# One row-maximum instruction over both score maps of a unit instead of two, in the first attention stage

## The reference, cut to what matters

```python
k1a, k2a = jnp.split(k_all, 2, axis=-1)
sa = DA ** -0.5
oa = attend(q1, k1a, v_all, sa) - lam.astype(hn.dtype) * attend(q2, k2a, v_all, sa)
# attend, per block of 128 queries:
s = jnp.einsum('bhqd,bhkd->bhqk', qblk, k).astype(jnp.float32) * scale
p = jax.nn.softmax(s, axis=-1).astype(v.dtype)
return jnp.einsum('bhqk,bhkd->bhqd', p, v)
```

## Time and profile before

| what | value |
|---|---|
| median of three runs | 2000.77 us (1998.8 to 2004.0) |
| span of the profiled execution | 2001.7 us |
| TensorE busy, whole span | 1921.7 us (96%) |
| VectorE busy, whole span | 1071.2 us (54%) |
| ScalarE busy, whole span | 717.5 us (36%) |
| the maxima of line 1415 | 60, of which 40 in the first attention stage |

### The profile page before, as it was taken

The page is one execution under the profiler, slowest core; times in us unless marked ns, Lnnn a source line. Parts: engine busy times, 40 slices in busy tenths (PEclk is TensorE's granted clock), DMA queues, the critical chain, the costliest instruction groups (busy, mean ns, idle before and its releaser), DMA issues.

```text
span 2001.7 us, 41374 instructions
## 1 busy us (share of the span) xinstructions
PE 1921.7 (96%) x18397; PEld 1700.8 (85%) x18397; DVE 1071.2 (54%) x1976; ACT 717.5 (36%) x1313; POOL 140.2 (7%) x138
## 2 busy tenths in 40 slices
PE   5998999999999999999999889999999999999997
PEld 2795444899999999999998678888659999999997
DVE  3226754475555563245475776766547555556223
ACT  2323554353333351133345744444214333334211
POOL 2000000000000000000001523322000000000000
PEclk7999999999999999999999999999899999999999
DMA  9123738312221223232221000000211222122322
GB/s 339 56 85 119 273 112 301 119 58 85 85 70 58 85 58 87 59 105 70 64 84 41 7 3 4 4 4 4 91 43 43 85 84 84 52 76 59 87 64 76
DMA packets 142065, 164.25 MB, mean 82 GB/s; under 512 B 2512, under 2 KB 107136, under 8 KB 141888
## 3 DMA queue, kind: packets, MB, share of 16 engines
q1 hardware_dynamic: 138736, 150.29, 23.3%
q0 software_dynamic: 3152, 11.32, 1.5%
HBM read 157.85 MB, written 3.75 MB: 81 GB/s over the span
## 4 chain that ended last, share of the span: by engine, by line
PE 87%; DVE 6%; DMA 2%; POOL 2%; ACT 1%; issue 1%; POOLq 0%; DVEq 0%; SPq 0%
PE ps L226 82%; DMA ring<-in_ada_w 2%; POOL work L2786 1%; PE ps L2422 1%; DVE ring L2671 1%; PE ps L1280 1%; DVE work L498 1%; POOL work L2788 1%; PE ps L347 1%; PE ps L2027 1%; DVE small L1415 0%; PE ps L2400 0%; PE ps L462 0%; DVE work L2689 0%; DVE work L2684 0%
## 5 line engine op out<-in xcount | busy, mean ns | idle before, releaser
L226 PE MATMUL ps<-x_hi_r,w_lo 128*128 128x320 f32 (+3 forms) x2240 | 519.7, 307 | 0.4 <-issue 0.4
L226 PE MATMUL ps<-x_hi_r,w_hi 128*128 128x320 f32 (+2 forms) x1792 | 428.9, 311 | 0.9 <-issue 0.9
L226 PE MATMUL ps<-x_lo_r,w_hi 128*128 128x320 f32 (+2 forms) x1792 | 424.9, 308 | 0.0
L226 PEld LDWEIGHTS ps<-x_hi_r,w_lo 128*128 128x128 f32 (+1 forms) x2240 | 372.4, 186 | 2.0 <-issue 0.5
L226 PEld LDWEIGHTS ps<-x_lo_r,w_hi 128*128 128x128 f32 x1792 | 305.6, 188 | 0.0
L226 PEld LDWEIGHTS ps<-x_hi_r,w_hi 128*128 128x128 f32 x1792 | 303.8, 188 | 1.4 <-issue 1.3
L226 PE MATMUL ps<-work 64*64 64x64 f32 (+9 forms) x3322 | 285.0, 281 | 17.0 <-ACT work L1344 6.7
L226 PEld LDWEIGHTS ps<-work 64*64 64x64 f32 (+5 forms) x3322 | 177.7, 152 | 97.6 <-issue 64.1
L678 DVE SCALAR_TENSOR_TENSOR work<-ps,par,work 128x511 f32<-128x511 f32 (+1 forms) x188 | 103.3, 550 | 254.5 <-ACT work L840 244.6
L840 ACT ACTIVATE work<-ps,par 128x640 f32<-128x640 f32 x88 | 78.0, 886 | 372.5 <-PE ps L226 372.5
L718 ACT ACTIVATE w_hi<-ring 128x1024 fp32r<-128x1024 f32 (+1 forms) x152 | 135.8, 938 | 206.9 <-DMA ring<-in_ffn_down 182.7
(11 more groups left out here) (383 smaller groups left out, 2534.1 us busy)
## 6 DMA issues: line engine op xcount, KB each, us to landing
ring<-in_ada_w SPq DMA_DIRECT2D x24, 2048.0 KB, 8.1
ring<-in_ffn_up SPq DMA_DIRECT2D x44, 1024.0 KB, 7.3
ring<-in_ffn_down SPq DMA_DIRECT2D x16, 1408.0 KB, 6.9
ring<-in_l_w_in SPq DMA_DIRECT2D x11, 1024.0 KB, 5.2
ring<-in_l_w_out SPq DMA_DIRECT2D x4, 2048.0 KB, 7.9
ring<-in_l_w_in SPq DMA_DIRECT2D x3, 2048.0 KB, 9.5
h<-in_xT POOLq DMA_DIRECT2D x1, 2560.0 KB, 14.7
out_yT<-work POOLq DMA_DIRECT2D x2, 768.0 KB, 4.0
```

Of the source, the lines that this page charges most:

```text
L226: return pe.matmul(out, lhsT, rhs, start=first, stop=last)
```

## The change

In the first attention stage one `tensor_reduce` takes the maxima of both maps of a unit: it reads PSUM as 128 x 2 x w (w is 640 or 128), reduces the innermost axis and writes two neighbouring columns of `small`, the same ones as before. It waits for the scores of both maps and raises the semaphore by two at its end. The waits on ScalarE stay as they are. In the second stage nothing changes.

```diff
+            def both_maxima(u):
+                w = NT if units[u][1] < 4 else P
+                dve.wait_ge(sg(x + "scores"), 2 * u + 2)
+                c = 32 + (2 * u % 4)
+                maps_at = ps_all[:, 0:2048].rearrange("p (s n) -> p s n", s=2)[:, :, 0:w]
+                dve.tensor_reduce(small[:, c:c + 2], maps_at, AXX, ALU.max, negate=True).then_inc(sg(x + "max"), 2)
+
...
             for u in range(len(units)):
-                maximum(u, 0)
                 if g == 0:
-                    maximum(u, 1)
+                    both_maxima(u)
                     weigh(u, 0)
                     weigh(u, 1)
                 else:
+                    maximum(u, 0)
                     weigh(u - 1, 0)
```

## The result

The changed kernel took 2010.57 us, median of four runs (2006.85 to 2011.73), against 2000.99 for four runs of the kernel before: ratio 1.0047, 95% interval 1.0034 to 1.006. It is slower by about 9.6 us; 8.4 were forecast. The time lies in the range.

The account below looks back on a forecast made before the run. A ring of three engines, once round per unit, was taken to bound the stage. Twelve latent units 8.04, unit 2 0.26 and unit 4 0.14 gave +8.4 us: 2000.77 + 8.4 = 2009.2, range 2004.8 to 2012.5.

Parts of the forecast that it names:

- The ring, and the first maximum on it: First stage: scores, maxima and exponentials go round three engines once per unit, 3.96 us; only the first maximum lies on the path.
- The duration: Time of the new joint maximum on VectorE: 1.49 us over 1280 columns, 0.42 us in context units.
- d: How much later a latent unit's first exponential starts: 1.49 - 0.82 = 0.67 us.
- The wait for both maps: Before the joint maximum: waiting for both maps' scores rather than the first's costs almost nothing.
- Unit 2: TensorE there waits for the ring's weights; 0.41 us of slack leaves 0.67 - 0.41 = 0.26 us of loss.
- Units 7, 12, 17, and 9, 14, 19: First three hidden by a ScalarE copy, by 0.05 us; 9 and 14 by TensorE's transposes; no scores follow 19.
- The sum: Loss over the first stage: 8.04 + 0.26 + 0.14 = +8.4 us, bounds +4.8 and +10.8.
- Rival B: Scores stand behind TensorE's own queue, so the lateness is hidden: not slower, 2000.8 us at full cover; chance 0.15.
- twelve uncovered units: Latent units 0, 1, 3, 5, 6, 8, 10, 11, 13, 15, 16, 18: 12 x 0.67 = 8.04 us.
- Rival C: VectorE's queue sets the period, so fewer instructions win 1.4 us: 1999.4 us, no measurable change; chance 0.03.
- Rival D: TensorE idles more, its granted clock falls to 0.94 in the stage, 4.9 us more: 2014.1 us; chance 0.07.
- A: The forecast itself: late first exponential in the first stage, +8.4 us, 2009.2 us; chance 0.75.

Follow-up runs that it names:

- The move of the copy: ScalarE copies the previous head's context result between the two exponentials of units 7, 12, 17: ratio 0.9998 on the kernel before, 1.0048 on the changed kernel.
- the filling: Changed kernel with the transposes of units 0 to 4 done twice (ratio 1.0072), then three times (one run, 2009.7 us).

## Why the prediction was right, step by step

*The ring, and the first maximum on it.* Shown. Taking the early signal away costs the loss by itself; taking the maximum twice costs another 1.53 us in every latent unit at the full clock. The engine that lost work, VectorE, lost it off the path.

*The duration.* 1.49 and 0.42 forecast, 1.492 and 0.416 measured. d = 0.67 held.

*The wait for both maps.* Mis-sized: "costs almost nothing" was 0.11 us in each latent unit, 0.04 for the second map's scores and 0.07 for the wait as an instruction of its own, which the raise by two brings. The prediction had read the end of the last matmul off a row, and those ends are modelled: 0.04 us can't be read there. I had read the cost of the change from the instruction that it adds and not from how it signals. Twelve units make 1.3 us of it.

*Unit 2.* 0.26 forecast, 0.41 in the first profile, and 0.78 where the weights come in time, as they did in the other profiles. Slack against a transfer was counted on from a single execution.

*Units 7, 12, 17, and 9, 14, 19.* Covered, as forecast; the first three by so little that the 0.11 us cost 0.05 each. The move of the copy shows what covers them.

*The sum.* +8.4 forecast, +10.0 in the stage at the full clock. What is missing is 12 x 0.11 = 1.3, 0.15 and 0.15. That the runs' 9.6 us lie so near the forecast is partly luck: the profiled stage grew by 11.2, and the six runs of the changed kernel again gave 12.2 (2011.8 against 1999.59). The range held them, but the room above +8.4 had been left for a longer instruction and a lower clock, not for a dearer wait.

*Rival B*, hidden behind TensorE: all twelve uncovered units paid in full. *Rival C*, the count of instructions: VectorE's 1.8 us bought nothing. The advice in Rules for kernel authors of the Trainium skill's page VectorE: DVE Perf Modes, fewer operations rather than fewer semaphores, stands there under chained operations, which the two maxima are not; VectorE's own time did fall with their number. Optimizing Scalar/DVE Operations in the Trainium skill's Perfetto Trace Analysis, by which breaking up instructions may let work be completed sooner, described the case: the one instruction instead of two cost 0.78 us a unit. *Rival D*, the clock: it was given 0.07 and a price of 4.9 us. It came in a small form, 1.2 us in the first profile, on top of A and not instead of it. I had treated the two as exclusive, and had looked only at the stage's own clock: the second layer, which I had left out, gave back 5.1 us in that profile, more than half of the forecast itself.

What stays open is what sets off the stretches at the lower clock in the first head. Of six profiles with one joint maximum in every unit five had them (the sixth was that with the transposes three times), and of six with two maxima in the first head, late signal or not, none had. Neither the unit's length nor TensorE's idle time ahead of unit 1's scores sorts them (2.47 us with the late signal, 2.48 in the changed kernel), the filling did not decide it, and with so few profiles chance is not ruled out.

## What to carry to other kernels

Before joining two instructions, look at who waits for the first of them alone: an early result that feeds a chain is worth its own instruction and its own signal, and the engine time that joining saves is worth nothing there unless that engine sets the period. Price a joined instruction with its signalling, not only its length: a wait for more, and a raise by more than one, have prices of their own. Units that have another wait ahead of the same consumer can be joined for next to nothing, and moving that other wait may be worth more than the join (here 1.6 us of the stage, too little for the runs to show).

## What the runs showed of the hardware

- A reduction of 128 x 2 x 640 from PSUM into two columns costs what a line through shorter ones gives, 1.492 us; the second row of the pattern and the second output have no visible price.
- With the semaphore raised by two, the wait ahead of the instruction became a separate one on VectorE's queue (20 of them, 21 ns each), and the maximum started 0.07 us later than with a raise by one.
- TensorE's granted clock over the stage was 1.00 with units of 3.95 us and with those of 4.68 us, 0.96 in the first profile with units of 4.73 us and 0.83 with units of 6.26 us; and the same 8137 matmuls of unchanged code took 338.0 us at a mean of 0.95 and 332.9 at 0.97.
